# First chunk after a norm or a merge: both output tiles per input tile, and one weight split moved ahead

## What is computed

```python
# first block (512 tokens)
merged = sigmoid(gate_a) * (o_a @ w_br_fox) + sigmoid(gate_c) * (o_c @ w_br_chunk)   # stage merge1
mix = merged @ w_out                                                                  # stage out1
x = layer_norm(alpha * x + (1 + g1) * mix, ln1_g, ln1_b)                              # LN_1
h = layer_norm(x) * (1 + sc2) + sh2                                                   # LN_MID
u = causal_depthwise_conv(h @ w_up, conv_w, conv_b); a, val = split(u)                # stage up1
y = (silu(a) * val) @ w_down                                                          # stage down1
x = layer_norm(alpha * x + (1 + g2) * y, ln2_g, ln2_b)                                # LN_2
# second block (16 meta tokens + 512)
h = h + 0.5 * swiglu(rmsnorm(h, ffn1_norm))                                           # up2, down2
...                                                                                   # attention, merge2
h = h + mixed @ w_out_2                                                               # stage out2
h = h + 0.5 * swiglu(rmsnorm(h, ffn2_norm))                                           # up3, down3
```

## Time and profile before

| | us |
|---|---|
| median of 3 runs (lowest, highest) | 2144.78 (2144.38, 2148.55) |
| the profiled execution: its time | 2148.04 |
| the profiled execution: its span | 2146.3 |
| PE busy, share of the span | 2034.6, 95% |
| DVE busy | 1004.7, 47% |
| ACT busy | 727.4, 34% |
| POOL busy | 24.3, 1% |
| mean granted TensorE clock | 0.976 |

### The profile page before, as it was taken

The page is one execution under the profiler, slowest core; times in us unless marked ns, Lnnn a source line. Parts: engine busy times, 40 slices in busy tenths (PEclk is TensorE's granted clock), DMA queues, the critical chain, the costliest instruction groups (busy, mean ns, idle before and its releaser), DMA issues.

```text
span 2146.3 us, 26565 instructions
## 1 busy us (share of the span) xinstructions
PE 2034.6 (95%) x10813; PEld 1697.0 (79%) x10813; DVE 1004.7 (47%) x1340; ACT 727.4 (34%) x948; POOL 24.3 (1%) x45
## 2 busy tenths in 40 slices
PE   5999999996999999989999999899999999999997
PEld 2788877873777778869999999688887787888885
DVE  7678753435555552254444322666323444444322
ACT  3444443423454442242222212445323332222211
POOL 0000000000000000000000000000000000000000
PEclk9999999998999999999999999999999999999999
DMA  6643213220222222312222222111112222222221
GB/s 264 213 148 128 99 40 119 98 98 0 79 90 105 78 79 89 105 40 98 78 98 81 79 94 89 71 59 40 42 59 97 86 91 85 91 98 92 82 94 65
DMA packets 34846, 195.43 MB, mean 91 GB/s; under 512 B 3680, under 2 KB 3696, under 8 KB 19552
## 3 DMA queue, kind: packets, MB, share of 16 engines
q1 hardware_dynamic: 29008, 173.55, 23.0%
q0 software_dynamic: 5776, 21.02, 2.9%
HBM read 192.46 MB, written 2.10 MB: 91 GB/s over the span
## 4 chain that ended last, share of the span: by engine, by line
PE 83%; DVE 10%; ACT 3%; issue 2%; DMA 1%; ACTq 0%; SPq 0%; DVEq 0%
PE PS L567 82%; DVE W_lo L1546 2%; ACT W_hi L1114 1%; PE PS L697 1%; DVE INV L1590 1%; DVE N L1595 1%; DMA A_low<-in_wada 1%; DVE T L1985 1%; DVE T L1976 1%; ACT L1114 1%; DVE A_high L2019 1%; ACT T L1114 0%; DMA ring<-in_wada 0%; ACT H_hi L1114 0%; DVE H_lo L1578 0%
## 5 line engine op out<-in xcount | busy, mean ns | idle before, releaser
L567 PE MATMUL PS<-H_hi,W_hi 128*128 128x512 f32 (+1 forms) x1976 | 634.3, 355 | 57.6 <-DVE H_lo L1578 20.5
L567 PE MATMUL PS<-H_hi,W_lo 128*128 128x512 f32 (+1 forms) x1976 | 635.0, 355 | 0.0
L567 PE MATMUL PS<-H_lo,W_hi 128*128 128x512 f32 (+1 forms) x1976 | 632.5, 354 | 0.0
L1546 DVE TENSOR_TENSOR W_lo<-W_raw,W_hi 128x2048 fp32r<-128x2048 f32 (+2 forms) x170 | 353.1, 2077 | 325.8 <-ACT W_hi L1114 325.2
L567 PEld LDWEIGHTS PS<-H_hi,W_hi 128*128 128x128 f32 x1976 | 351.6, 192 | 121.2 <-issue 42.8
L1114 ACT ACTIVATE W_hi<-W_raw 128x2048 fp32r<-128x2048 f32 (+2 forms) x170 | 295.5, 1738 | 322.1 <-PE PS L567 321.3
L567 PEld LDWEIGHTS PS<-H_hi,W_lo 128*128 128x128 f32 x1976 | 351.0, 192 | 49.8 <-issue 0.2
L567 PEld LDWEIGHTS PS<-H_lo,W_hi 128*128 128x128 f32 x1976 | 350.1, 191 | 50.0 <-issue 0.2
L567 PE MATMUL PS<-G_hi,W_hi 128*128 128x512 f32 (+1 forms) x704 | 209.6, 338 | 1.3 <-DVE W_lo L1546 1.3
L567 PE MATMUL PS<-G_hi,W_lo 128*128 128x512 f32 (+1 forms) x704 | 210.2, 339 | 0.0
L567 PE MATMUL PS<-G_lo,W_hi 128*128 128x512 f32 (+1 forms) x704 | 209.3, 338 | 0.0
(11 more groups left out here) (246 smaller groups left out, 2169.4 us busy)
## 6 DMA issues: line engine op xcount, KB each, us to landing
W_raw<-in_wts SPq DMA_DIRECT2D x119, 1024.0 KB, 4.7
W_raw<-in_wdown SPq DMA_DIRECT2D x48, 704.0 KB, 4.0
ring<-in_wada POOLq DMA_DIRECT2D x32, 512.0 KB, 3.8
A_high<-in_wada SPq DMA_DIRECT2D x6, 1024.0 KB, 18.0
A_low<-in_wada SPq DMA_DIRECT2D x2, 1024.0 KB, 10.8
X<-in_xT SPq DMA_DIRECT2D x2, 1024.0 KB, 10.4
X<-in_xT POOLq DMA_DIRECT2D x1, 2048.0 KB, 9.0
out<-N SPq DMA_DIRECT2D x8, 256.0 KB, 2.1
```

Source lines behind the costliest of these rows:

```text
L567: return nc.tensor.matmul(*a, **kw)
L1546: vector.tensor_tensor(W_lo[:, c.odd, 0:size], W_raw[:, c.odd, 0:size], W_hi[:, c.odd, 0:size].bitcast(FP32), ALU.subtract).then_inc(w_lo, 1)
```

## The change

`walk` gets an argument `ahead`: the first round stands outside the loop and leaves out the split of the stage's second chunk. `up_first` of ACT and DVE uses it. That split now stands ahead of `norm(LN_1)` on ACT, and in the `between` hook of `norm(LN_1)` on DVE. In `project`, a chunk with `ready` runs through the input tiles once, and does both output tiles for each.

```diff
-        def walk(eng, split, s, n, per, body, after_first=None):
+        def walk(eng, split, s, n, per, body, after_first=None, ahead=False):
...
-            def chunks_of_round(i, step, size_after):
+            def chunks_of_round(i, step, size_after, skip=False):
                 for k in range(per):
                     nxt = At(s.c + k + 1, step, i)
                     size = s.words[0] if k < per - 1 else size_after
-                    if size:
+                    if size and not (skip and k == 0):
                         split(nxt, size)
...
             first = 0
+            if ahead:
+                chunks_of_round(0, per, s.words[0], True)
+                first = 1
...
                 chunk_ready(c)
                 group_free(s, b)
+                if ready is not None:
+                    for k in range(KT):
+                        tile_ready(ready, k)
+                        for m in range(tiles):
+                            a = (k * tiles + m) * P
+                            wh, wl = W_hi[:, c.odd, a:a + P], W_lo[:, c.odd, a:a + P]
+                            for n, (w, x) in enumerate(((wh, act_hi), (wh, act_lo), (wl, act_hi))):
+                                for o, (t0, tn) in outs_of(b, m, tok, at):
+                                    last = mm(o, w, x[:, k, t0:t0 + tn], start=k == 0 and n == 0, stop=k == KT - 1 and n == 2)
+                    last.then_inc(w_used, 1)
+                    return
                 for m in range(tiles):
...
-                    last = feature_tile(outs_of(b, m, tok, at), c.odd, m * P, tiles * P, range(KT), act_hi, act_lo,
-                                        ready=ready if m == 0 else None)
+                    last = feature_tile(outs_of(b, m, tok, at), c.odd, m * P, tiles * P, range(KT), act_hi, act_lo)
...
-                walk(act, split, s, FH, 2, body)
+                walk(act, split, s, FH, 2, body, ahead=True)
...
             scale_residual("out1", 2, 2)
+            split(At(st["up1"].c + 1), WC)
             norm(LN_1)
             norm(LN_MID)
...
-                walk(dve, split, s, FH, 2, body)
+                walk(dve, split, s, FH, 2, body, ahead=True)
...
-            norm(LN_1)
+            norm(LN_1, between=lambda: split(At(st["up1"].c + 1), WC))
             norm(LN_MID)
```

## The result

The change takes the kernel from 2145.65 to 2125.12 us (medians of four runs each): ratio 0.9902, 95% interval 0.9885 to 0.9919. The profiled execution took 2125.81 us with a span of 2124.0. One execution of the last experiment (e9), of 9761.58 us, is left out of its ratio, and nothing here explains it.

A forecast was written before the change was run, and what follows sets the result against it. PE was taken as the bound, 83% of the chain's span. Savings of 4.1 + 4.3 + 2.4 + 0.5 = 11.3 us took the profiled 2148.04 to 2136.7, or the median 2144.78 to 2133.5 us; range 2129 to 2140.

The forecast's parts named there:

- Out1 and out2: First chunks of both out stages: the M_lo wait and half-clock matmuls behind it go, saving 4.1 and 4.3 us.
- Up1's first chunk: PE no longer outruns DVE's tiles after the first wait; saves 2.4 us, including 0.7 from the early split.
- Up3: First chunk of up3: PE is busy through all 11.20 us, so nothing is saved.
- The order's own cost: Alternating banks in the five first chunks costs zero, bounded by 0 to 2.4 us over 5 x 48 matmuls.
- rival D: Five first chunks: alternating banks costs PE its clock, 41 us more, 2186 us; chance 0.04.
- Up2: First chunk of up2: PE, behind the tiles until tile 6, saves 0.5 us.
- B: Out stages' second chunks start no sooner, the wait moves there; only 2.9 us gained, 2141.9 us; chance 0.06.
- C: The early split pushes LN_1 by 1.9 us on ACT and 2.3 on DVE; 7.1 us gained, 2137.7; chance 0.05.
- A: Only standstills go, 8.0 us; half-clock matmuls of the out chunks come back elsewhere; 2136.8 us; chance 0.14.
- The early split: Up1's second-chunk split in LN_1: ACT's 1.9 and DVE's 2.29 us hidden, 2.1 us to spare on DVE; cost 0.

The follow-up runs named there:

- e9: Kernel before plus the changed project and a one-element SiLU ahead of up1's loop; no peeled round, no split moved: 2125.96 us, ratio 0.9908.
- e4: Kernel before plus a one-element SiLU on ACT ahead of up1's loop, nothing of the change: 2134.66 us, ratio 0.9953.
- e6: Kernel after plus a one-element square root ahead of SiLU in each up1 round: 2125.52 us, ratio 0.9913.
- e2: Kernel after with the old project, so only the early split and the peeled round: 2134.79 us, ratio 0.9948.
- e7: Kernel after with the split of the third chunk of up2 and up3 moved ahead of the late norm's root: 2117.83 us, ratio 0.9872.
- e5: Kernel after plus a one-element square root behind G_hi in each up1 round: 2139.92 us, ratio 0.9977.

## Why the prediction was wrong

The direction and the mechanism of part 1 were right; the time lies outside the range, since a gain of the same size in part 2 was missed. By its steps:

- **Out1 and out2** (4.1 and 4.3 us): measured 4.10 and 4.34. M_lo's slack and that of the second chunk held. e4 shows what of it is the clock's: there PE stands the same 2.40 us, the clock doesn't fall behind it, and out1 takes 48.2 instead of 49.6 us, out2 46.2 instead of 47.9. So a removed wait of this kind is worth 2.7 us (48.20 - 45.50) where the clock stays up and 4.1 to 4.3 where it falls.
- **Up1's first chunk** (2.4): 2.3. **Up3** (0): 11.15 us before and 11.14 after. **The order's own cost** (0): 48 matmuls in 10.87 us at clock 1.00, so nothing; rival D is out. The Trainium skill's rule on going round the PSUM banks (TensorE: Matmul & The Clock Gate, "A second HAM failure mode: psum-queue depth-cycling") speaks of small idle times between groups of matmuls; in this chunk PE has none, and so the rule had nothing to act on here.
- **Up2** (0.5): 0.9. Its first chunk takes 13.92 us instead of 14.80; it takes 13.45 to 14.08 in the eight profiles with the new order, and 14.75 to 14.80 in the three without. The whole stage doesn't show it: it takes 266.4 to 268.8 us in the nine profiles of before to e6 and e9, with the same work at other granted clocks.
- **The other rivals.** B and C are out: no wait stands ahead of a second chunk of an out stage, and INV comes 4.5 us behind the last subtraction, against 4.4. A, that the clock takes its share back elsewhere, shows only in part: the out chunks kept their 4.1 and 4.3 us, and 1.0 us came back in up3.
- **The early split**: hidden, as forecast. DVE still idles before it inverts, in the row below, 2.22 us instead of the 4.42 in the earlier trace rows; 2.1 had been forecast.

```profile
496.18 2.28 DVE L1560 TENSOR_TENSOR W_lo<-W_raw,W_hi 128x2048 fp32r<-128x2048 f32 x1
...
500.69 3.35 DVE L1604 RECIPROCAL INV<-DEV 128x512 f32<-128x512 f32 x1 [2.22 <-ACT DEV L1127]
```

- **The step that failed** is "The peeled round adds instructions to the code of ACT and DVE, none to the work. I take 0, between -0.5 and 2.3 us." It took work away: two table loads per round of up1, of which the one between G_hi and W_hi lay on the chain to the next W_lo. In place of 0 the runs show -10.3 us, all in up1: 243.9 to 233.5 us for the rest of the stage after against before, and the whole stage 10.3 shorter in e2, 10.4 in e4. With it fell "the waits for W_lo in the up stages hang on PE's own end of the chunk before, so they move with it". They do hang on it, by a chain of ACT and DVE work of 12.1 us (from about 558.30, where PE starts the chunk before, to the end of W_lo at 570.40) against about 11.1 us of matmuls, and the change took 1.4 us out of that chain. The prediction had left the nine equal waits, which are among the 13 of the earlier trace rows, as they were because the diff didn't seem to touch them, and never priced the chain behind them. It could have: the load was in the rows of the round, and 45 loads in the list of ACT's groups.
- **The reckoning.** 4.1 + 4.3 + 2.3 + 0.9 + 10.3 = 21.9 us against 20.5 between the medians. The profiled pair differs by 22.2 us of span: the attention stage at its other clock gives 4.6 more, and the stretch ahead of out1 (1.7 us longer), the rest of up2 (1.3), up3 (1.0) and the norms ahead of up1 (0.3) take 4.3 back. In up3 the clock stayed low for longer behind the wait for W_lo: 0.72 over the 10 us behind it after, 0.83 before. The stage is longer so in each profile with part 1 up to e6 and in e9. Why the clock there goes with part 1 is open; no run was made for it. e7 removes that wait, and up3 then takes 245.55 us.
- **A slip in rival D.** Up3's term is 22.2 - 11.2 = 11.0, not 11.1; the sum stays 41.

## What to carry to other kernels

Before costing a change to a loop's shape at nothing, look for activation table loads inside the loop: here one stood at its head in every round, and one tiny activation of the loop's own function ahead of the loop removed it. When many equal short waits stand in the list, write down the chain behind one of them against the time that covers it; place decides, for the same loads cost 14 us at one point of the round and nothing at another. Compare the number of instructions of each engine before and after: that row led to the cause here. And where PE stands about 2.4 us, the clock may take more: 1.4 and 1.7 us in the out stages here, 4.6 and 6.0 over the attention stage, or nothing.

## What the runs showed of the hardware

A table load shows 1.28 us busy, and added 1.41 us to the way from one activation to the next, since the neighbours no longer overlap; in e5 the way from G_hi to W_hi is 2.48 us with load and the small root. The Trainium skill (ScalarE: Activation LUTs, "What ACT_TABLE_LOAD costs") gives 1283 ns for the load, which the rows confirm, and a drain on top that makes 2.66 us of each switch; the trace shows no more than the 1.41.

After one and the same wait of 2.40 us PE went on at half clock in some executions and at full in others (out1: 49.6 us before and 49.7 in e2, 48.2 in e4). The attention stage took 273.8 to 274.0 us in eight profiles and 278.4 and 279.9 in two, with the same matmuls; an edit far ahead of a stage can go with a move from the one to the other, which gives or takes more than many an edit is worth. That the edit causes the move is not shown, with one profile each.
